# Delta rule of a fused two-layer block: keys turned once instead of twice, and the inverted blocks scattered by one transpose and two masked copies

## The reference, cut to what matters

```python
q = l2_normalize(qkv[..., :W].reshape(shp))          # k alike
g_cum = jnp.cumsum(g, axis=-1)
decay_incl = jnp.exp(jnp.where(incl, diff, NEG))
k_beta = k * beta[..., None]
lmat = jnp.einsum('bhncd,bhnjd->bhncj', k_beta, k) * decay_strict
a_mat = lmat + jnp.eye(C)
sol = lax.linalg.triangular_solve(a_mat, rhs, left_side=True, lower=True, unit_diagonal=True)
...
k_dec = ki * jnp.exp(g_last[..., None] - gi)[..., None]
state = state * jnp.exp(g_last) + jnp.einsum('bhcd,bhce->bhde', k_dec, v_new)
```

## Time and profile before

| | |
|---|---|
| median of 3 runs | 848.8 us (848.28 to 850.86) |
| the profiled execution's own time | 849.63 us |
| its span | 847.8 us |
| PE busy | 824.1 us (97%), 6592 matmuls |
| DVE busy | 617.3 us (73%) |
| ACT busy | 486.7 us (57%) |
| POOL busy | 67.6 us (8%) |
| chain that ended last | PE 86%, DVE 6%, ACT 3%, DMA 3% |

### The profile page before, as it was taken

The page is one execution under the profiler, slowest core; times in us unless marked ns, Lnnn a source line. Parts: engine busy times, 40 slices in busy tenths (PEclk is TensorE's granted clock), DMA queues, the critical chain, the costliest instruction groups (busy, mean ns, idle before and its releaser), DMA issues.

```text
span 847.8 us, 17630 instructions
## 1 busy us (share of the span) xinstructions
PE 824.1 (97%) x6592; PEld 766.4 (90%) x6592; DVE 617.3 (73%) x1051; ACT 486.7 (57%) x899; POOL 67.6 (8%) x70
## 2 busy tenths in 40 slices
PE   6999999999999999998999999999999999999997
PEld 3899988889999998987898788999999999999885
DVE  4497876677889766977776669674778887888543
ACT  3444565476699565583656457565647554455434
POOL 1000001400001002143000011000002030000000
PEclk9999999999999999999999999999999999999999
DMA  9999965704552131543544425434455454545521
GB/s 374 379 378 391 372 250 192 265 6 151 191 198 91 62 103 56 191 161 130 206 150 149 149 76 182 153 138 150 172 202 188 161 184 163 184 167 194 199 100 49
DMA packets 22012, 153.85 MB, mean 181 GB/s; under 512 B 2496, under 2 KB 2752, under 8 KB 3904
## 3 DMA queue, kind: packets, MB, share of 16 engines
q1 hardware_dynamic: 20592, 145.69, 47.1%
q0 software_dynamic: 1360, 7.34, 2.4%
HBM read 151.97 MB, written 1.05 MB: 180 GB/s over the span
## 4 chain that ended last, share of the span: by engine, by line
PE 86%; DVE 6%; ACT 3%; DMA 3%; issue 1%; SPq 0%; DVEq 0%; ACTq 0%
PE ps L391 44%; PE ps L1242 7%; PE ps L486 7%; PE ps L464 4%; PE ps L425 3%; DVE w_lo L1921 2%; PE ps L434 1%; PE ps L825 1%; PE ps L456 1%; DVE work L2144 1%; DMA raw<-in_moba_first 1%; ACT w_hi L1282 1%; DMA proj<-in_ada_first 1%; PE ps L560 1%; PE ps L583 1%; DMA memkv<-in_ada_first 1%
## 5 line engine op out<-in xcount | busy, mean ns | idle before, releaser
L1921 DVE TENSOR_TENSOR w_lo<-raw,w_hi 128x1024 fp32r<-128x1024 f32 x230 | 284.3, 1242 | 93.8 <-ACT w_hi L1282 92.3
L1282 ACT CAST w_hi<-raw 128x1024 fp32r<-128x1024 f32 (+1 forms) x230 | 239.5, 1049 | 162.6 <-PE ps L391 65.1
L391 PE MATMUL ps<-in_hi,w_hi 128*128 128x256 f32 x1120 | 161.2, 286 | 1.3 <-ACT core_a L1369 1.3
L391 PE MATMUL ps<-in_lo,w_hi 128*128 128x256 f32 x1120 | 157.2, 283 | 0.0
L391 PE MATMUL ps<-in_hi,w_lo 128*128 128x256 f32 x1120 | 157.2, 283 | 0.0
L391 PEld LDWEIGHTS ps<-in_hi,w_hi 128*128 128x128 f32 x1120 | 144.4, 191 | 6.0 <-issue 2.8
L391 PEld LDWEIGHTS ps<-in_hi,w_lo 128*128 128x128 f32 x1120 | 144.5, 192 | 0.0
L391 PEld LDWEIGHTS ps<-in_lo,w_hi 128*128 128x128 f32 x1120 | 144.4, 192 | 0.0
L2186 DVE SCALAR_TENSOR_TENSOR proj<-work,params,proj 128x256 f32 (+1 forms) x72 | 35.5, 493 | 8.0 <-ACT proj L1496 1.8
L1998 DVE SCALAR_TENSOR_TENSOR work<-raw,cs,work 128x1024 f32 x24 | 30.8, 1285 | 4.8 <-DVE w_lo L1921 1.6
L1242 PE MATMUL ps<-w_hi,in_hi 128*128 128x512 f32 x88 | 34.2, 389 | 0.0
(11 more groups left out here) (426 smaller groups left out, 1343.5 us busy)
## 6 DMA issues: line engine op xcount, KB each, us to landing
raw<-in_mixed SPq DMA_DIRECT2D x24, 1024.0 KB, 6.9
raw<-in_ffn_up SPq DMA_DIRECT2D x22, 1024.0 KB, 4.8
raw<-in_gdn_in SPq DMA_DIRECT2D x16, 1024.0 KB, 4.8
raw<-in_w_in SPq DMA_DIRECT2D x16, 1024.0 KB, 4.8
raw<-in_merge SPq DMA_DIRECT2D x12, 1024.0 KB, 4.8
raw<-in_ffn_down SPq DMA_DIRECT2D x11, 1024.0 KB, 4.7
raw<-in_branch SPq DMA_DIRECT2D x6, 1024.0 KB, 4.8
raw<-in_moba_out SPq DMA_DIRECT2D x4, 1024.0 KB, 6.8
```

The lines of the kernel that those rows point to most:

```text
L391: mm = pe.matmul(half(u, 0), w[:, u, k * P:(k + 1) * P], a[:, base + k, :], start=(n == 0 and k == 0), stop=(n == 2 and k == UNIT - 1))
L1282: act.copy(w_hi[:, u, :], src).then_inc(hi_done, 1)
L1921: dve.tensor_tensor(w_lo[:, u, :], src, w_hi[:, u, :].bitcast(F32), ALU.subtract).then_inc(lo_done, 1)
```

## The change

Keys are turned once. `natural_k(g)` stays, and right behind `lengths(g)` ACT now scales the same PSUM bank by the decay (`decayed_k(g)`), with the column `kcol[:, 0]` made earlier: its subtraction and copy move from DVE to POOL, its exponential to the front of ACT's stage. `natural_k(2)` and `natural_k(3)` now wait for `decayed_k(0)` and `decayed_k(1)`, since they reuse the banks; `z_unit(25)` stands ahead of them. `natural_k_again` is gone. The inverted blocks are transposed in one instruction over 128 partitions into a new area `turned` (the place of the scratch area `product`), and two copies with a mask per partition (columns 4 and 5 of `parity`) put them into the left and right half of `tt`: one on DVE, one on ACT. They write all of `tt`, so that its memset on POOL goes.

```diff
@@ build
+    turned = area(2560, MATS, 32, of=core_b)
@@ PE: natural_k
-                pe.wait_ge(*after("gdn_length", g - 1))
+                pe.wait_ge(*after("gdn_kdg", 4 * (g - 1)))
@@ PE: order
         z_unit(24)
+        z_unit(25)
         natural_k(2)
         natural_k(3)
-        z_unit(25)
         for g in range(4):
             gram_k(g)
         z_unit(26)
         pe.wait_ge(*after("gdn_lt", 4))
-        pe.wait_ge(*after("gdn_length", 4))
+        pe.wait_ge(*after("gdn_kdg", 12))
...
         z_unit(27)
-        natural_k_again(0)
-        natural_k_again(1)
         z_unit(28)
-        natural_k_again(2)
-        natural_k_again(3)
         z_unit(29)
...
         pe.wait_ge(*after("gdn_kdg", MATS))
-        pe.wait_ge(*after("gdn_scattered", 4))
+        pe.wait_ge(*after("gdn_scattered", 3))
@@ ACT
-        for g in range(4):
+        act.wait_ge(*after("gdn_kx", 2))
+        link(act.activation(kcol[:, 0, :], kcol[:, 0, :], ACT.Exp))
+        for g in range(2):
+            lengths(g)
+            decayed_k(g)
+        for g in (2, 3):
             lengths(g)
...
         for g in range(4):
             decay(g)
-        act.wait_ge(*after("gdn_kx", 2))
-        act.activation(kcol[:, 0, :], kcol[:, 0, :], ACT.Exp).then_inc(sem("gdn_root"), 1)
+        for g in (2, 3):
+            decayed_k(g)
         z_out(24)
...
         z_out(27)
-        for g in range(4):
-            decayed_k(g)
         z_out(28)
         z_out(29)
+        act.wait_ge(*after("gdn_scattered", 1))
+        act.activation(tt[:, :, 32:64], turned, ACT.Copy, scale=parity(5)).then_inc(sem("gdn_scattered"), 1)
@@ DVE
-        dve.tensor_tensor(kcol[:, 0, 0:8], gcol[:, 32:40], gcol[:, 0:8], ALU.subtract).then_inc(sem("gdn_kx"), 1)
-        dve.tensor_copy(kcol[:, 0, 8:16], gcol[:, 8:16]).then_inc(sem("gdn_kx"), 1)
...
-        dve.wait_ge(*after("gdn_zero", 2))
-        for b in range(4):
-            r = slice(32 * b, 32 * b + 32)
-            dve.transpose(tt[r, :, 32 * (b % 2):32 * (b % 2) + 32].rearrange("p m (h c) -> p c h m", h=2),
-                          gathered[r].rearrange("p c (h m) -> p c h m", h=2)).then_inc(sem("gdn_scattered"), 1)
+        dve.transpose(turned.rearrange("p m (h c) -> p c h m", h=2),
+                      gathered[:].rearrange("p c (h m) -> p c h m", h=2)).then_inc(sem("gdn_scattered"), 1)
+        dve.wait_ge(*after("gdn_scattered", 1))
+        dve.tensor_scalar(tt[:, :, 0:32], turned, parity(4), None, ALU.mult).then_inc(sem("gdn_scattered"), 1)
@@ POOL
-        pool.memset(tt, 0.0).then_inc(sem("gdn_zero"), 1)
...
+        pool.wait_ge(*after("gdn_col_done", 1))
+        pool.tensor_tensor(kcol[:, 0, 0:8], gcol[:, 32:40], gcol[:, 0:8], ALU.subtract).then_inc(sem("gdn_kx"), 1)
+        pool.tensor_copy(kcol[:, 0, 8:16], gcol[:, 8:16]).then_inc(sem("gdn_kx"), 1)
```

More of the change, by code:

```diff
@@ L102 @@
 CONSTS = [("ident", P), ("one", P), ("neg", 3 * P), ("back", 3 * P), ("upper", P), ("colmask", S),
-          ("pick", 31), ("parity", 4)]
+          ("pick", 31), ("parity", 6)]
 CCOL = {}
@@ L1567, in decayed_k @@
         def decayed_k(g):
-            act.wait_ge(*after("gdn_natk", 4 + g + 1))
             for j in range(4):
-                act.activation(kdg[:, 4 * g + j, :], ps[:, 2 + g, j * P:(j + 1) * P], ACT.Copy,
+                act.activation(kdg[:, 4 * g + j, :], ps[:, 2 + g % 2, j * P:(j + 1) * P], ACT.Copy,
                                scale=column(0, 4 * g + j)).then_inc(sem("gdn_kdg"), 1)
@@ L1599, in _ @@
         z_out(26)
-        act.wait_ge(*after("gdn_root", 3))
+        act.wait_ge(*after("gdn_root", 2))
         for g in range(4):
@@ L1627, in _ @@
             act.copy(pm[:, mats(s), :], blocks(s)).then_inc(sem("gdn_ps"), 1)
-        act.wait_ge(*after("gdn_scattered", 4))
+        act.wait_ge(*after("gdn_scattered", 3))
         for n in range(2):
@@ L2245, in _ @@
         low("gdn_in", 28)
-        dve.wait_ge(*after("gdn_zero", 4))
+        dve.wait_ge(*after("gdn_zero", 3))
         dve.wait_ge(*after("gdn_packed", 1))
@@ L2659, in _ @@
         pool.memset(ct, 0.0).then_inc(sem("gdn_zero"), 1)
-        pool.memset(tt, 0.0).then_inc(sem("gdn_zero"), 1)
         pool.memset(inverse, 0.0).then_inc(sem("gdn_zero"), 1)
-        pool.wait_ge(*after("gdn_zero", 3))
+        pool.wait_ge(*after("gdn_zero", 2))
         pool.memset(inverse.rearrange("p (d s) -> p d s", s=17)[:, :, 0:1], 1.0).then_inc(sem("gdn_zero"), 1)
+        pool.wait_ge(*after("gdn_col_done", 1))
+        pool.tensor_tensor(kcol[:, 0, 0:8], gcol[:, 32:40], gcol[:, 0:8], ALU.subtract).then_inc(sem("gdn_kx"), 1)
+        pool.tensor_copy(kcol[:, 0, 8:16], gcol[:, 8:16]).then_inc(sem("gdn_kx"), 1)
         for g in range(4):
@@ L2698, in _constants @@
     even = np.where(np.arange(P) % 32 < 16, 1.0, 0.0)
+    first = np.where(np.arange(P) % 64 < 32, 1.0, 0.0)
     out = {
@@ L2706, in _constants @@
         "upper": np.where(j >= i, 0.0, NEG),
-        "parity": np.stack([-even, even - 1.0, even, 1.0 - even], 1),
+        "parity": np.stack([-even, even - 1.0, even, 1.0 - even, first, 1.0 - first], 1),
     }
```

## The result

The changed kernel takes 852.46 us (median of 13 executions, 850.9 to 854.94) beside 849.04 us of the kernel before (13, 848.28 to 851.9): ratio 1.0034, 95% interval 1.0022 to 1.0047. Run once more against before at the end of the study it gave 1.0023 (1.0013 to 1.0032). It is slower: by 2.9 us going by the first ratio and by 2.0 going by the second (1.1 to 4.0 with both intervals), and the two medians above are 3.4 us apart. Forecast were 2.7 us (+0.32%) and 851.5 us, range 848.4 to 853.6; the median lies 1.0 us above the 851.5. The profiled execution took 850.9 us, its span is 849.1 us, the shortest of the 13, and shows only 1.3 us of the loss.

The account below looks back on a forecast made before the run. PE, busy 97%, bounds the kernel, with ACT's full queue nearly level: ACT 4.0 us late, less 0.7 slack at unit 29, less 0.63 wait at tp, gives +2.7 us, median 851.5 us (+0.32%), range 848.4 to 853.6.

Parts of the forecast that it names:

- PE's wait at unit 26: Unit 26 waits for ACT's copy of unit 24, 4.0 us later behind eight scaled keys: a new 3.8 us gap.
- rival 3: ACT's interleaved work or the copies behind it run 1 to 2 us shorter: net +0.5 to +1.5, 849.8 us; 14%.
- second hold: Unit 29 waits for ACT's copy of unit 27, at 278.06 instead of 274.04, and starts at 278.7.
- first hold: PE's unit 26 waits for ACT's copy of unit 24, at 264.85 instead of 260.83, and starts at 265.35.
- The gains: 1.58 us less PE work (second turning of keys), 2.8 us less DVE tail; together they buy only 0.63 us.
- rival 4: The full DVE transpose costs four times its old piece, 4.4 us: tp +3.7, 852.5 us; 3%.
- Rival 1: Shortened chains win if unit 24's copy is ready by 261.5: tp -1.3 to -2.2, median 847.5 to 846.6; 9%.
- The first fall: Half clock behind the gap at unit 26 costs 1.7 us of PE work, hidden because ACT sets unit 29.
- the fall at the gate products: After the gap at 392.0 to 394.8 us, clock 0.50 for 3.4 us: 1.7 us of PE work lost.
- rival 2: Lower clock during unit 29 and `gram_q`, or a later fall, adds 1.7 us: 853.2 us; 16%.
- The size: tp (matmuls of L942) starts at 283.6 instead of 280.91, +2.7 us, with nothing after it absorbing the shift.

Follow-up runs that it names:

- Experiment 3: Changed kernel with ACT's copy of unit 24 moved between the squares and scaled keys of groups 1 and 2: 852.39 us, ratio 1.0036 against the kernel before.
- experiment 4: Experiment 3 with the copy of unit 27 also moved, between the second and third group of scaled values: 849.59 us, ratio 1.0002 against the kernel before.
- experiment 1: Kernel before with the new scatter alone (one transpose over 128 partitions, two masked copies), keys still turned twice: 849.77 us, ratio 1.000.
- experiment 10: Experiment 9's kernel with the old scatter (four transposes of 32 partitions): 850.34 us, ratio 1.0014 against the kernel before.
- Experiment 9: Experiment 5's kernel with the copy of unit 25 ahead of the silu of the values, quarter blocks ahead of ACT's masked copy: 847.73 us, ratio 0.9974.
- experiment 7: Changed kernel with five matmuls of 256 columns filling PE's gap ahead of the gate products: 851.22 us, ratio 1.0017 against the kernel before.
- experiment 5: Experiment 3 with ACT's work in order of need, and PE's unit 27 ahead of turning the values: 850.18 us, ratio 1.0007 against the kernel before.
- Experiment 6: Kernel before with five matmuls of 256 columns filling PE's gap ahead of the gate products: 849.86 us, ratio 1.0001.
- experiment 2: Changed kernel with the old scatter (four transposes of 32 partitions, tt zeroed on POOL): 854.74 us, ratio 1.0051 against the kernel before.

## Why the prediction was right

*PE's wait at unit 26.* Forecast 3.8 us, measured 3.4; the copy of unit 24 forecast at 264.85, measured 265.00. Counted from unit 24 the sum over ACT's instructions held within 0.2 us, since they are the same instructions as in the earlier trace rows and ACT had nothing to wait for but the turned keys; that excludes rival 3, which needed 1 to 2 us less there. Experiment 3 takes this wait away and nothing is won, as the prediction's second hold (unit 29 by the copy of unit 27) says; experiment 4 takes that away too and the time comes back. The two together show what the trace of one kernel can't: that the second hold alone suffices for the loss, and that ACT's copies, with all its other work left in place, are what PE waited for. What the first hold would cost alone, with the copy of unit 27 early and that of unit 24 late, wasn't run; by the prediction's sum it is less, since PE reaches unit 29 at 277.0 without a fall of the clock.

*The gains.* 1.58 us of PE work and 2.8 of DVE's buy only 0.63. Shown for the scatter by experiment 1 (nothing) and, reversed, by experiment 10: once ACT is in order, the same edit is worth 2.6 us, 2.25 of them at tp. The transposition was priced at 1.1 us, measured 1.09, which excludes rival 4; the masked copy at 0.49, measured 0.48. Of ACT's masked copy the prediction said 0.6 us and that it is in time; it took 0.72 and was (it ended at 283.08, tp started at 283.73), but in experiment 1 it took 1.00 and was the last to arrive.

*Rival 1 (the shortened chains win)* fell for this order, and its premise, an early copy of unit 24, was too weak: experiment 3 gave it that and won nothing. Experiment 9 shows the sum that it hoped for, -1.95 us at tp, but only with copies 24, 25 and 27 ahead of the bulk work.

*The clock.* The first fall is hidden, as forecast (experiments 3 and 7). Two things were missed. The prediction's sum took the fall at the gate products as given in both kernels. It isn't: five of ten profiled executions had it, at 1.5 us each, beside 2.0 to 2.9 us that the change costs, and the one execution that was profiled happened to have it before and not after. The other executions agree as far as their mean clock tells: in the 35 of before beside experiment 5, nine at 0.999 took 848.7 us on average and 21 at 0.997 took 850.5. Experiment 6, which took this fall away, didn't lower the median, so that it isn't the only thing that spreads the times. And rival 2 has a true part: a spell twice as long at unit 26 makes unit 29 0.95 us later in experiment 2's profile. The changed kernel's three executions at 0.993 and less took 854.06 to 854.94 us; that they had this spell is inferred, since none of them was profiled.

*The size.* tp moved by 2.49 us counted from unit 24, 2.8 by the clock of the trace, for 2.7 forecast; by the two ratios the whole moved 2.0 to 2.9 us. Nothing after tp absorbed it: from tp to the gate products it is 113.93 us before and 113.83 after. At tp the mechanism and its size were right; that the whole agrees as closely is in part luck, since how many executions had the fall at the gate products moves a median by up to 1.5 us.

## What to carry to other kernels

Work that is moved forward on a full engine is paid by everything it is put in front of; look first for short instructions that free a buffer (here copies of 0.35 us out of a bank) and keep them ahead of bulk work. When a wait is seen, remove it and look whether the end moves: a second hold that is as late may stand behind it. And before one profile is set beside another, compare their granted clocks: a fall that came in one and not in the other can be as large as the change.

## What the runs showed of the hardware that wasn't expected

A gap in PE's work of 2.2 to 2.6 us ahead of the gate products was followed by a spell of 3.4 us at half clock in five of ten profiled executions and not in the other five, and the gap's length doesn't separate them; each spell cost 1.5 us at the end. Gaps of that size ahead of tp did the same, one with a spell (2.17 us, experiment 10) and one without (2.20 us, experiment 2). After the gap of 3.4 us at unit 26 there was a spell in all four profiled executions that had the gap (3.4 us long in three, 6.8 in one). The Trainium skill (TensorE: Matmul & The Clock Gate, the table of rules) asks for no long idle gaps between bursts of matmuls, because one throws the clock back to half. The traces agree for the gap at unit 26, and show besides that gaps about 1 us shorter can do it in some executions. A DVE transpose of 128x512 took 1.09 us (1.15 in experiment 1) and one of 32x512 took 1.04 to 1.12: four times the partitions cost no more time.
